# The third block of the output projection taken up by input rows, between the last attention jobs

## The reference, cut to what matters

```python
h = modulate(rmsnorm(x, norm_gain[i, 0]), sh1, sc1)
y = mixer(h) # for swa, fox and b2: attention(h @ w_in) @ w_o
x = x + g1[:, None, :] * y
h = modulate(rmsnorm(x, norm_gain[i, 1]), sh2, sc2)
x = x + g2[:, None, :] * swiglu(h, ffn_w_gu[i], ffn_w_down[i])
```

## Time and profile before

| what | value |
|---|---|
| median of three runs | 1752.36 us (1751.1 to 1758.9) |
| the profiled execution | 1752.58 us |
| its span | 1750.7 us |
| mean granted TensorE clock | 0.969 of full speed |
| TensorE matmul busy | 92% |
| VectorE, ScalarE, GpSimd busy | 69%, 45%, 5% |

### The profile page before, as it was taken

The page is one execution under the profiler, slowest core; times in us unless marked ns, Lnnn a source line. Parts: engine busy times, 40 slices in busy tenths (PEclk is TensorE's granted clock), DMA queues, the critical chain, the costliest instruction groups (busy, mean ns, idle before and its releaser), DMA issues.

```text
span 1750.7 us, 30753 instructions
## 1 busy us (share of the span) xinstructions
PE 1608.9 (92%) x12542; PEld 1525.3 (87%) x12542; DVE 1199.8 (69%) x1592; ACT 788.3 (45%) x1030; POOL 88.9 (5%) x109
## 2 busy tenths in 40 slices
PE   0877899989989999989999999979999989999998
PEld 0766899989879999988889999858999979889998
DVE  4997687766546877673468776865877668666665
ACT  1443334345534334355454333554343357655453
POOL 0032000000100000001100000020000002300000
PEclk9988899989979999999999999999999999999999
DMA  8764597664405887653339876432978555335550
GB/s 338 296 226 160 239 385 305 247 264 157 157 4 214 360 311 290 231 199 121 134 108 372 311 299 235 187 121 84 364 305 304 213 207 181 121 130 185 190 177 39
DMA packets 54219, 383.75 MB, mean 219 GB/s; under 512 B 6256, under 2 KB 6512, under 8 KB 8448
## 3 DMA queue, kind: packets, MB, share of 16 engines
q1 hardware_dynamic: 49824, 359.55, 54.6%
q0 software_dynamic: 4320, 23.14, 3.7%
HBM read 378.47 MB, written 4.19 MB: 219 GB/s over the span
## 4 chain that ended last, share of the span: by engine, by line
PE 80%; DVE 11%; DMA 4%; ACT 3%; issue 2%; POOL 1%; SPq 0%; DVEq 0%; ACTq 0%
PE PS L1647 65%; PE PS L1668 4%; DVE wlo L1166 3%; DVE adar L1180 3%; PE PS L1694 2%; DMA adar<-ada 2%; DMA raw<-weights 2%; PE PS L1767 2%; ACT whi L772 1%; PE PS L1793 1%; DVE XN L1219 1%; DVE NM L1324 1%; PE PS L1814 1%; DVE SCR L1318 1%; PE PS L1770 1%
## 5 line engine op out<-in xcount | busy, mean ns | idle before, releaser
L1647 PE MATMUL PS<-hhi,whi 128*128 128x256 f32 x2568 | 741.4, 289 | 28.8 <-DVE hlo L1212 23.8
L1166 DVE TENSOR_TENSOR wlo<-raw,whi 128x2048 fp32r<-128x2048 f32 x234 | 537.0, 2295 | 289.9 <-ACT whi L772 289.9
L1647 PE MATMUL PS<-hlo,whi 128*128 128x256 f32 x2568 | 733.2, 286 | 0.0
L1647 PE MATMUL PS<-hhi,wlo 128*128 128x256 f32 x2568 | 732.5, 285 | 0.0
L772 ACT ACTIVATE whi<-raw 128x2048 fp32r<-128x2048 f32 x234 | 446.5, 1911 | 521.7 <-PE PS L1647 460.7
L1647 PEld LDWEIGHTS PS<-hhi,whi 128*128 128x128 f32 x2568 | 499.7, 195 | 46.3 <-issue 40.4
L1647 PEld LDWEIGHTS PS<-hlo,whi 128*128 128x128 f32 x2568 | 500.1, 195 | 1.3 <-issue 1.2
L1647 PEld LDWEIGHTS PS<-hhi,wlo 128*128 128x128 f32 x2568 | 499.5, 195 | 0.0
L1180 DVE CUSTOM_DVE_ANT_0 adar<-adar,CB 128x1024 f32<-128x1024 f32 x240 | 286.4, 1233 | 21.3 <-DMA adar<-ada 21.2
L1647 PE MATMUL PS<-ahi,whi 128*128 128x256 f32 x936 | 266.8, 285 | 5.1 <-DVE wlo L1166 4.0
L1647 PE MATMUL PS<-alo,whi 128*128 128x256 f32 x936 | 266.0, 284 | 0.0
(11 more groups left out here) (215 smaller groups left out, 1347.5 us busy)
## 6 DMA issues: line engine op xcount, KB each, us to landing
raw<-weights SPq DMA_DIRECT2D x234, 1024.0 KB, 6.5
adar<-ada SPq DMA_DIRECT2D x104, 1024.0 KB, 5.5
adar<-ada POOLq DMA_DIRECT2D x16, 1024.0 KB, 5.4
bias_rows<-acc POOLq DMA_DIRECT2D x12, 256.0 KB, 3.2
adar<-bias_rows POOLq DMA_DIRECT2D x8, 256.0 KB, 3.2
CST<-cst_in SPq DMA_DIRECT2D x1, 1128.0 KB, 11.9
CB<-c_in SPq DMA_DIRECT2D x2, 512.0 KB, 4.6
X<-x_in SPq DMA_DIRECT2D x1, 1024.0 KB, 8.5
```

What stands on the lines that cost most here:

```text
L1166: v.tensor_tensor(wlo[:, u % CV, :], raw[:, u % RAW, :], whi[:, u % CV, :].bitcast(F32), ALU.subtract).then_inc(lo_done, 1)
L1647: m = pe.matmul(o, w(a), h(b), start=first and k_ == 0, stop=last and k_ == 2, skip_group_check=True)
```

## The change

Block 2 is no longer multiplied in one go behind `out_part(7)`. A new function `third_part(p)` multiplies row p into it (six matmuls, bank 4), and its calls stand between the last jobs: parts 0 to 5 before `out_part(7)`, parts 6 and 7 behind it. The first one waits until `mask_max(7)` has read the score banks. In the two swa layers `values(6)`, `transposes(7)` and `values(7)` also move ahead of one `out_part` each. Block 3 is multiplied as before, after the last part. The gla layer is untouched, and so are the lists of all other engines.

```diff
+                def third_part(p):
+
+                    u = plan.uout[l] + 2
+                    if p == 0:
+                        pe.wait_ge(s_masked, pos0[l] + PAIRS)
+                        unit_ready(u)
+                    for t in range(2):
+                        m = mixed_part(u, p, IB[2], t, p == 0 and t == 0, p == PAIRS - 1)
+                    if p == PAIRS - 1:
+                        m.then_inc(pe_unit, 1)
...
                     values(5)
                     transposes(6)
                     out_part(3)
+                    for p in range(3):
+                        third_part(p)
+                    values(6)
                     out_part(4)
-                    values(6)
+                    third_part(3)
+                    transposes(7)
                     out_part(5)
-                    transposes(7)
+                    third_part(4)
+                    values(7)
                     out_part(6)
-                    values(7)
+                    third_part(5)
                     out_part(7)
 
                 if kind == "fox":
...
                     out_part(4)
+                    third_part(0)
+                    third_part(1)
                     transposes(7)
                     out_part(5)
+                    third_part(2)
+                    third_part(3)
                     values(7)
                     out_part(6)
+                    third_part(4)
+                    third_part(5)
                     out_part(7)
 
                 if kind == "b2":
...
                     values(6)
+                    third_part(0)
+                    third_part(1)
+                    third_part(2)
                     transposes(7)
                     out_part(5)
+                    third_part(3)
                     values(7)
                     out_part(6)
+                    third_part(4)
+                    third_part(5)
                     out_part(7)
...
-                    for i in range(2, OUT_UNITS):
-                        unit_ready(plan.uout[l] + i)
-                        for t in range(2):
-                            for p in range(PAIRS):
-                                m = mixed_part(plan.uout[l] + i, p, IB[i], t, p == 0, p == PAIRS - 1)
-                        m.then_inc(pe_unit, 1)
+                    third_part(6)
+                    third_part(7)
+                    unit_ready(plan.uout[l] + 3)
+                    for t in range(2):
+                        for p in range(PAIRS):
+                            m = mixed_part(plan.uout[l] + 3, p, IB[3], t, p == 0, p == PAIRS - 1)
+                    m.then_inc(pe_unit, 1)
```

## The result

The changed kernel takes 1768.62 us, the median of six runs (1764.88 to 1771.85). The kernel before takes 1756.07 us (1751.1 to 1758.9) in six runs, of which three are those of the forecast. The ratio is 1.0081, with a 95% interval of 1.0062 to 1.01: slower, by 12.55 us between the medians, where 11.85 us were forecast. The time itself lies 0.6 us above the range of the prediction.

A forecast was written before the change was run, and what follows sets the result against it. TensorE was taken as the bound (80% of the chain), except at the first layer's end, on ScalarE and VectorE. Idle time and delay of 9.45 us plus 2.4 for the clock, added to 1752.36, gave 1764.2 us; range 1757 to 1768.

The forecast's parts named there:

- A part's price, 0.72 us: TensorE's third parts of block 2: six matmuls 0.12 us apart, so 0.72 us for each part.
- Block 3 ready 5.28 us after the start of `out_part(7)`, a new wait of 2.4 us: TensorE before block 3: only 2.88 us of matmuls cover its split; 2.5 us idle with the slow first matmul.
- X of block 3 some 0.3 us late on VectorE, hidden: VectorE behind `out_part(7)`: X3 some 0.3 us late, but `sum_squares` needs it only in its last quarter.
- Fourth layer: the wait before `out_part(7)` is filled: Fourth layer: 2.5 us new idle, less the 0.95 us wait and its 0.1 us slow first matmul: +1.45 us.
- Those three with the clock: 2.5 + 2.5 + 1.45 + 2.4 = 8.85 us: Later layers: fox and b2 +2.5 us each, fourth layer +1.45, and +2.4 for lost clock.
- First layer 3.0 us, its chain unchanged in length: First layer: VectorE's chain starts with the delayed `out_part(7)` and gets no shorter, so +3.0 us.
- Clock: half of three falls at 1.6 us: Block 3 in three layers: new waits may drop the clock, up to 4.8 us; half taken, +2.4 us.
- the split isn't late: Rival, block 3: split ends within 2.9 us of `out_part(7)`'s start, leaving only the first layer's 3.0: 1754.4 us; chance 0.08.
- the first layer absorbs its delay: Rival, first layer: VectorE's later work doesn't follow `out_part(7)`, so 3.0 us go: 1761.2 us; chance 0.08.
- the clock gives it back: Rival, norms behind changed layers: shifted norms keep the high clock more often, up to 1.6 us each: 1760.2 us; chance 0.12.
- the eight norm waits that the prediction counted: TensorE's norm waits of about 2.3 us: four of eight followed by the low clock, the basis for half.
- the last of the sum: Base plus difference: 11.85 us added to the kernel's median of 1752.36 us, giving 1764.2 us.

The follow-up runs named there:

- experiment 1: The changed kernel with only parts 0 and 1 of block 2 before `out_part(7)`, the rest behind: 1755.86 us, ratio 0.9999 to the kernel before.
- experiment 2: The changed kernel with only half the columns of block 3 split in the four attention layers, the rest left out: 1756.7 us, ratio 1.0002 to the kernel before.
- experiment 4: The kernel before with the new order in fox, the fourth layer and b2, not in the first layer: 1764.27 us, ratio 1.0052.
- experiment 3: The kernel before with the new order in the first layer alone: 1759.99 us, ratio 1.0016.
- experiment 6: The changed kernel with block 3 split in two halves and multiplied row by row, nothing left out: 1760.06 us, ratio 1.003 to the kernel before.

## Why the prediction was right in its steps and wrong in its number

- **A part's price, 0.72 us.** Right: 0.12 us a matmul behind `out_part(7)` in experiment 1, and between the jobs in the changed kernel's timeline.
- **Block 3 ready 5.28 us after the start of `out_part(7)`, a new wait of 2.4 us.** Right: 5.27, and 2.2 us in all four layers as the profile counts it, from the end of the last matmul. Experiments 1 and 2 show the cause from both sides, by more cover and by a shorter split.
- **X of block 3 some 0.3 us late on VectorE, hidden.** Off, without effect: VectorE was free 0.1 us before the block ended in fox, and 1.6 us in the fourth layer, where the low clock made the block longer.
- **Fourth layer: the wait before `out_part(7)` is filled.** Right: the row for line 1358 of the earlier trace rows is gone. The mark there moved by 2.95 us, which is the 1.45 of the forecast and 1.5 of clock. b2 moved by 4.0, which is 2.5 and 1.5. In fox the end moved by only 0.9, since the stretch behind its wait of 1.85 us (before 867.75, and before 876.24 in the changed kernel) had a mean granted clock of 0.88 in the profile of before and 1.00 in this one; medians, not this one execution, weigh the three together.
- **Those three with the clock: 2.5 + 2.5 + 1.45 + 2.4 = 8.85 us.** Measured 7.9 to 9.1 (experiment 4).
- **First layer 3.0 us, its chain unchanged in length.** Right: 15.62 us both times, and 2.8 to 3.6 us (experiment 3).
- **Clock: half of three falls at 1.6 us.** Right as a number: five of nine, at 1.5 us (7.50 less 6.01). Partly this is luck. The half came from waits at another place, the norms', and it is made of none in fox and all in b2; which block falls was not told, and isn't understood. The count of the norms was also one short: the first layer's wait of 2.35 us, at 174.27, was followed by the low level as well, five of nine. The Trainium skill, "TensorE: Matmul & The Clock Gate", on HAM oscillation, shows bursts of matmuls that start at the half clock again behind DMA waits of some 3 to 5 us; here waits of 2.2 us were followed by it in five cases of nine.
- **Rivals.** That the split isn't late fell with the new waits. That the first layer absorbs its delay fell with experiment 3, whose interval begins at 1.0, so that it says this weakly, but whose shift in the chain says it plainly. That the clock gives it back did not happen: the differences of medians came out at 12.55 and 11.9 us against 9.45 without any clock. Of the eight norm waits that the prediction counted, four were followed by the low level in the kernel before, and six of the same eight in each of the three profiles with the new order in the later layers. In these executions the clock took more at the norms, not less; the medians leave little room for it as a regular cost, and no run takes it apart.

**The step that failed is the last of the sum: "so I add to the median: 1752.36 + 11.85 = 1764.2 us".** The addend holds; the base doesn't. The median of three runs was taken as the kernel's time, with support from a profiled execution "0.2 us from the median", which is only one more draw. In 32 and 23 runs the same kernel has a median of 1756.41 and 1756.2 us and goes from 1750 to 1762. On that base the sum is 1756.2 + 11.85 = 1768.1 us; measured were 1768.62 and 1768.13. The range failed for the same reason: its upper end, 1768, was built from the costs of the mechanisms alone, a full set of clock falls, and kept nothing for the base. Three runs from a spread of 12 us leave their median several us unsure: of all triples that can be drawn from these 55 runs, 95% have a median between 1751.6 and 1760.2 us, and 7% one of 1752.36 or less. The three at hand, 1751.1 to 1758.9, showed 7.8 us of that spread already.

## What to carry to other kernels

Work that is moved ahead of the instruction which frees a buffer takes away the cover of whatever refills that buffer: count the time from the release to the refilled buffer (here 5.3 us) and leave at least so much of the engine's own work behind it. Fill a wait with as much work as it holds and no more: `out_part` calls moved into the waits, with two third parts ahead of `out_part(7)` in the swa layers, one in fox and none in b2, turned 12 us lost into 9 us won; which of the moves earned it was not taken apart. When a forecast is a base and a difference, give the base its own share of the range, by the spread of the runs that it comes from.

## What the runs showed of the hardware

- One kernel's executions lie 12 us apart (1750 to 1762 us over 32 runs), 0.7%, and the changed kernel's profiled execution was 18.2 us longer in span than a profile of before that sits at the low end. Marks in the two chains put some 4 us of it on stretches that the change doesn't touch and that ran at another granted clock (the 120 matmuls behind one norm of fox take 14.52 us in one and 17.24 us in the other), and 2.65 us on the start of the first layer and a wait for GpSimd there.
- A wait of 2.2 us of TensorE in front of the same 48 matmuls is followed by 2.4 GHz or by 1.2 GHz, and this changes from one execution to another for the same place: 6.02 and 7.50 us for the fourth layer. After waits of 0.3 us no block 3 ran long in the profiles of experiments 2 and 6, six blocks in all.
- ScalarE's and VectorE's split shortens almost with its width: 1.93 to 1.07 us and 2.30 to 1.24 us from 2048 to 1024 columns, each with its end signalled. Back to back, as in experiment 6, the two halves take 2.01 us on ScalarE and 2.36 us on VectorE, where one whole instruction takes 1.91 and 2.29, so cutting it in two costs 0.1 us or less on each engine.
